# A decoder block on one core: ten of eleven tile pairs of the second feed-forward product in a seven-product form, in two passes, with the weight sums on GpSimd

## The reference

```python
def swiglu_ffn(x, g, w_in, w_out):
    h = rmsnorm(x, g)
    gate, up = jnp.split(h @ w_in, 2, axis=-1)
    return x + (jax.nn.silu(gate) * up) @ w_out        # hidden width 2816, w_out is 2816 x 1024
```

## Time and profile before

| | before |
|---|---|
| median of 3 runs | 900.63 us (900.39 to 900.72) |
| profiled execution | 900.4 us, its span 898.7 us |
| TensorE busy | 888.4 us (99%) |
| VectorE busy | 596.2 us (66%) |
| ScalarE busy | 385.7 us (43%) |
| GpSimd busy | 57.5 us (6%) |
| mean granted TensorE clock | 0.999 |

### The profile page before, as it was taken

The page is one execution under the profiler, slowest core; times in us unless marked ns, Lnnn a source line. Parts: engine busy times, 40 slices in busy tenths (PEclk is TensorE's granted clock), DMA queues, the critical chain, the costliest instruction groups (busy, mean ns, idle before and its releaser), DMA issues.

```text
span 898.7 us, 13165 instructions
## 1 busy us (share of the span) xinstructions
PE 888.4 (99%) x5292; PEld 793.1 (88%) x5292; DVE 596.2 (66%) x711; ACT 385.7 (43%) x555; POOL 57.5 (6%) x59
## 2 busy tenths in 40 slices
PE   9999999999999999999999999999999999999997
PEld 7998888889999998988888888899999999888886
DVE  5685666789577678755466476998888887433333
ACT  5654432345444444523244332554555445322223
POOL 0111000000000000024100053000000000000000
PEclk9999999999999999999999999999999999999999
DMA  9946332213322222672211122222322233322212
GB/s 350 364 168 265 110 105 94 94 47 99 137 93 95 94 100 89 226 289 94 92 49 51 44 94 107 81 95 97 127 103 93 93 116 117 117 93 94 94 48 94
DMA packets 16091, 108.17 MB, mean 120 GB/s; under 512 B 1840, under 2 KB 1968, under 8 KB 4016
## 3 DMA queue, kind: packets, MB, share of 16 engines
q1 hardware_dynamic: 13408, 93.99, 28.3%
q10 hardware_dynamic: 2176, 12.00, 3.5%
q0 software_dynamic: 464, 1.57, 0.5%
HBM read 101.26 MB, written 6.29 MB: 120 GB/s over the span
## 4 chain that ended last, share of the span: by engine, by line
PE 84%; DVE 10%; ACT 4%; issue 2%; DMA 1%; SPq 0%; POOLq 0%; POOL 0%; ACTq 0%; DVEq 0%
PE psum L1445 28%; PE psum L1447 27%; PE psum L1446 27%; DVE blk L870 2%; ACT blk L395 1%; DVE sig L1155 1%; DMA pack<-first 1%; DVE tl L870 1%; DVE wl L870 1%; DVE raw L1061 1%; DVE raw L1059 1%; DVE raw L1060 1%; DVE merged L1158 0%; ACT wh L395 0%; PE psum L1697 0%
## 5 line engine op out<-in xcount | busy, mean ns | idle before, releaser
L1445 PE MATMUL psum<-th,w7h 128*128 128x256 f32 x504 | 142.7, 283 | 0.3 <-ACT snap L395 0.3
L1447 PE MATMUL psum<-th,w7l 128*128 128x256 f32 x504 | 142.6, 283 | 0.0
L1446 PE MATMUL psum<-tl,w7h 128*128 128x256 f32 x504 | 142.6, 283 | 0.0
L870 DVE TENSOR_TENSOR wl<-raw,wh 128x2048 fp32r<-128x2048 f32 (+1 forms) x44 | 89.4, 2043 | 50.0 <-ACT wh L395 49.9
L1445 PEld LDWEIGHTS psum<-th,w7h 128*128 128x128 f32 x504 | 96.8, 192 | 0.6 <-issue 0.5
L1446 PEld LDWEIGHTS psum<-tl,w7h 128*128 128x128 f32 x504 | 96.8, 192 | 0.0
L1447 PEld LDWEIGHTS psum<-th,w7l 128*128 128x128 f32 x504 | 96.8, 192 | 0.0
L395 ACT ACTIVATE wh<-raw 128x2048 fp32r<-128x2048 f32 (+1 forms) x44 | 73.1, 1675 | 20.8 <-PE psum L1447 19.5
L1445 PE MATMUL psum<-hh,wh 128*128 128x512 f32 x192 | 75.0, 391 | 0.0
L1447 PE MATMUL psum<-hh,wl 128*128 128x512 f32 x192 | 74.7, 389 | 0.0
L1446 PE MATMUL psum<-hl,wh 128*128 128x512 f32 x192 | 74.7, 389 | 0.0
(11 more groups left out here) (265 smaller groups left out, 2197.3 us busy)
## 6 DMA issues: line engine op xcount, KB each, us to landing
raw<-weights SPq DMA_DIRECT2D x79, 1024.0 KB, 4.8
pack<-first SPq DMA_DIRECT2D x3, 768.0 KB, 7.9
vraw<-weights SPq DMA_DIRECT2D x2, 1024.0 KB, 12.1
xt<-xt SPq DMA_DIRECT2D x1, 2048.0 KB, 18.7
X<-x SPq DMA_DIRECT2D x2, 1024.0 KB, 27.7
X<-x ACTq DMA_DIRECT2D x1, 2048.0 KB, 10.1
memt<-memt SPq DMA_DIRECT2D x1, 1024.0 KB, 22.6
kv_store<-kh ACTq DMA_DIRECT2D x1, 1024.0 KB, 3.9
```

The costliest lines, as they stand in the source:

```text
L870: return V.tensor_tensor(dst, v, f32(hi), ALU.subtract)
L1445: nc.tensor.matmul(dst, lh, rh, start=start, stop=False, **kw)
L1446: nc.tensor.matmul(dst, lh, rl, start=False, stop=False, **kw)
L1447: return nc.tensor.matmul(dst, ll, rh, start=False, stop=stop, **kw)
```

## The change

Of the eleven pairs, ten (`NP`) are now done in the seven-product form. For a pair, the 512 tokens are cut into halves of 256 and the 1024 columns into halves of 512, so that both the hidden values (two tiles x two halves of tokens) and the weights (two tiles x two halves of columns) are 2 x 2 blocks. Each product is 256 tokens x 128 x 512 columns: two output tiles x three matmuls, 42 matmuls for a pair. The results of the seven products need more room than PSUM has, so there are two passes over the ten pairs. Pass one does three products for every pair, into banks 4 and 5, 6 and 7, 0 and 1; pass two does the other four. Between and behind the passes, sums are kept in SBUF (`kept`) and added back (`merge_part`). The eleventh pair runs as before, with other bank numbers, once `fo_merged` says that its bank has been put together.

The weights are stored as four blocks per pair (`out_blocks`). Pass one loads the first three blocks, pass two the last three, 768 KB each time. GpSimd makes two sums of 128 x 512 for each pair and pass, in `raw` and in `t2` (`t2_early`, `t2_late`), 40 in all. The high and low parts are made in smaller pieces. VectorE also makes two sums of hidden values (128 x 256) per pair and pass.

The residual's 32 transposes now go into banks 2 and 3 during pass one, and ScalarE copies six of the eight results into `xres`; the last two stay in the banks. In the mixer's gates, the fourth `merge` of a half moves behind `gate_prep`. Semaphores of single use are joined into counting ones (`squares_ready`, `var_ready`, `rstd_ready`).

```diff
@@ GpSimd @@
+            for i in range(NP):
+                n = FO0 + i
+                w = raw[:, n % SLOTS, :]
+                pool.wait_ge(landed[n % SLOTS], landing(n))
+                nc.gpsimd.tensor_tensor(w[:, S:2 * S], w[:, S:2 * S], w[:, 0:S], ALU.subtract).then_inc(fo_sums, 1)
+                if i == 2:
+                    pool.wait_ge(panel_done, FO0)
+                    pool.dma_start(gf[:], gf_in.to_broadcast([P, D])).then_inc(gf_here, 16)
+                pool.wait_ge(fo_sums, 2 * i + 1)
+                nc.gpsimd.tensor_tensor(t2(i), w[:, 2 * S:3 * S], w[:, S:2 * S], ALU.subtract).then_inc(fo_sums, 1)
+            for i in range(NP):
+                n = FB0 + i
...
+                nc.gpsimd.tensor_tensor(w[:, 0:S], w[:, 3 * S:4 * S], t2(i), ALU.subtract).then_inc(fo_sums, 1)
+                nc.gpsimd.tensor_tensor(w[:, S:2 * S], w[:, 2 * S:3 * S], w[:, S:2 * S], ALU.subtract).then_inc(fo_sums, 1)
@@ ScalarE @@
+            def first_pass_hi(i):
+                p = i % SLOTS
+                act.wait_ge(hid_ready, 2 * i + 2)
+                act.wait_ge(panel_done, FO0 + i - 1)
+                copy(hsh[p][:, 0, 0:Q], hid[:, 2 * i, 0:Q]).then_inc(hid_first_hi, 1)
+                act.wait_ge(fo_sums, 2 * i + 1)
+                copy(foh[p][:, 0:2 * S], raw[:, p, 0:2 * S]).then_inc(fo_first_hi, 1)
...
+            def second_pass_hi(i):
+                p = i % SLOTS
+                act.wait_ge(panel_done, FB0 + i - 1)
+                copy(hsh[p][:, 1, :], hid[:, 2 * i + 1, :]).then_inc(hid_first_hi, 1)
+                act.wait_ge(fo_sums, 2 * NP + 2 * i + 2)
+                copy(foh[p][:, 0:2 * S], raw[:, p, 0:2 * S]).then_inc(fo_first_hi, 1)
@@ VectorE, gates @@
                 merge(h - 1, 2)
+                gate_prep(n + 1, i + 1)
                 merge(h - 1, 3)
-                gate_prep(n + 1, i + 1)
                 gate_prep_lo(n + 1, i + 1)
@@ VectorE @@
+            def first_pass_lo(i):
+                p = i % SLOTS
+                dve.wait_ge(hid_first_hi, i + 1)
+                lo(hsl[p][:, 0, 0:Q], hid[:, 2 * i, 0:Q], hsh[p][:, 0, 0:Q]).then_inc(hid_first_lo, 1)
+                chain(V.tensor_tensor(hid[:, 2 * i, Q:S], hid[:, 2 * i, Q:S], hid[:, 2 * i + 1, Q:S], ALU.add))
+                V.tensor_tensor(hid[:, 2 * i, 0:Q], hid[:, 2 * i, Q:S], hid[:, 2 * i, 0:Q], ALU.subtract).then_inc(hid_sums, 1)
+                dve.wait_ge(fo_first_hi, i + 1)
+                lo(fol[p][:, 0:2 * S], raw[:, p, 0:2 * S], foh[p][:, 0:2 * S]).then_inc(fo_first_lo, 1)
...
@@ TensorE @@
+            for i in range(NP):
+                p, last = i % SLOTS, i == NP - 1
+                done = fo_part if last else None
+                pe.wait_ge(hid_first_lo, i + 1)
+                pe.wait_ge(fo_first_lo, i + 1)
...
+                out_product(4, p, 0, 0, start=i == 0, signal=done)
+                pe.wait_ge(hsl_ready, i + 1)
+                out_product(6, p, 2, 1, start=i == 0, signal=done)
+                pe.wait_ge(lo_ready, FO0 + i + 1)
...
+                out_product(0, p, 1, 2, start=i == 0, signal=done, closing=True).then_inc(panel_done, 1)
```

More of the change, by code:

```diff
@@ L69 @@
 FO0 = FI0 + HT
-PANELS = FO0 + HT // 2
+NP = 10
+FB0 = FO0 + NP
+FC0 = FB0 + NP
+PANELS = FC0 + 1
 C_MEM, C_MIX, C_X, C_FFN = 0, 8, 16, 24
@@ L827, in _ @@
[L827 to L831 removed]
+            flat = lambda t: t[:].rearrange("p a b -> p (a b)")
+            def first_pass_hi(i):
[5 more added lines that the diff above has]
+                copy(foh[p][:, 0:2 * S], raw[:, p, 0:2 * S]).then_inc(fo_first_hi, 1)
@@ new lines, in second_pass_rest_hi, with keep_part @@
+            def second_pass_rest_hi(i):
+                p = i % SLOTS
+                copy(foh[p][:, 2 * S:4 * S], raw[:, p, 2 * S:4 * S]).then_inc(hi_ready, 1)
+                act.wait_ge(hid_sums, NP + i + 1)
+                copy(hsh[p][:, 0, :], hid[:, 2 * i, :]).then_inc(hsh_ready, 1)
+            def keep_part(which, product, src):
+                for m in range(2):
+                    act.wait_ge(*part_done(product, m))
+                    copy(kept[:, which, m, :], bank[src + m]).then_inc(fo_kept, 1)
@@ L1419, in _, with merge_part @@
+            def merge_part(b, product, which, m, kept_by=0):
+                dve.wait_ge(*part_done(product, m))
+                if kept_by:
+                    dve.wait_ge(fo_kept, kept_by)
+                src = kept[:, which, m, :] if which is not None else xres[:, m, :]
+                V.tensor_tensor(bank[b], bank[b], src, ALU.add).then_inc(fo_merged, 1)
             add_kept(0, NS - 2)
-            fo_lo(0)
+            first_pass_lo(0)
             strassen_product(0, NS - 2, hid[:, HT - 2, :])
@@ L1806, in _ @@
                 strassen_panel(it * 2 + 1, 1)
[L1808 to L1832, removed]
-                        elif n == HT // 2 - 1:
-                            ins.then_inc(fo_tile, 1)
@@ new lines, in out_product @@
+            def out_product(banks, p, a, w, start=False, signal=None, free=None, closing=False):
+                h, g = hsh[p][:].rearrange("p a b -> p (a b)"), hsl[p][:].rearrange("p a b -> p (a b)")
+                c = slice(w * S, (w + 1) * S)
+                for m in range(2):
+                    if free:
+                        pe.wait_ge(free[0], free[1] + m)
+                    r = slice(a * Q + m * P, a * Q + (m + 1) * P)
+                    ins = mm3(bank[banks + m], h[:, r], g[:, r], foh[p][:, c], fol[p][:, c], start, signal is not None, skip_group_check=True)
+                    if signal and not (m == 1 and closing):
+                        ins.then_inc(signal, 1)
+                return ins
```

262 lines of the change are left out of this document (197 added, 65 removed).

## The result

| | before | after |
|---|---|---|
| median | 900.61 us (900.39 to 900.72) | 910.37 us (910.18 to 912.53) |
| profiled execution | 900.4 us, its span 898.7 us | 910.2 us, its span 908.4 us |
| TensorE busy, matmuls | 888.4 us, 5292 | 885.2 us, 5232 |
| VectorE busy, instructions | 596.2 us, 711 | 677.4 us, 825 |
| GpSimd busy | 57.5 us | 126.2 us |

The ratio is 1.0114, 95% interval 1.0097 to 1.0132: the change makes the kernel 1.1% slower, clear of the noise. 60 matmuls are gone, 13.6 us at their rate, but TensorE's busy time falls by 3.2 us only. A matmul shows 0.39 us and starts every 0.227 us, so short gaps between them count as busy.

What follows compares the result with a forecast made beforehand. Before, TensorE's matmul count and issue rate bound the kernel; after, VectorE, held by GpSimd's sums, bounds the last stage. Stage 10.3 us longer less 1.6 in the gates, 8.7 us on 900.4: 909 us, range 897 to 918.

Steps and rivals of the forecast that it cites:

- 60 matmuls less are 13.6 us, if nothing holds TensorE.: Last stage, ten pairs: 48 matmuls become 42 each, 60 x 0.227 = 13.6 us less for TensorE.
- VectorE stands still for 1.10 us per sum.: Last stage: each GpSimd sum reading SBUF holds VectorE's two-input instructions 1.10 us, 2.20 us a pair and pass.
- No hold: Rival, last stage: GpSimd's sums barely hold VectorE, TensorE sets the pace; 885 to 893 us, about 887; chance 0.15.
- a short hold: Rival, last stage: a sum holds VectorE only 0.84 us, 9.4 us less, about 900 us; chance 0.12.
- I counted 36: Last stage: the number of GpSimd sums by which the prediction scaled the length of a hold on VectorE.
- VectorE becomes the bound in both passes, 5.69 and 6.38 us a pair.: Last stage: VectorE's work plus 2.20 us of holds exceeds TensorE's 4.09 us (pass one) and 5.45 us (pass two).
- VectorE over 90% busy: Sign that the hold is real: VectorE over 90% busy from 771 to 886 us.
- The stage is 10.3 us longer.: Last stage: TensorE begins the last of ten pairs at 885.7, ends 892.3; the eleventh began at 882.0 before.
- The gates gain 1.6 us.: Mixer's gates: moving the fourth merge behind gate_prep removes TensorE's three waits for `gsnap`, 1.6 us in total.
- The slot's round does not bind.: Last stage: landing, GpSimd sums, ScalarE copy and VectorE part take 8.2 us and waits, against 11.4 for two pairs.
- waits that end with a landing: Sign of being wrong: TensorE's waits ending with a DMA landing would mean the slot's round binds.
- GpSimd comes last: Rival, last stage: sums run only once VectorE has run dry; 8 us more, 917 us; chance 0.13.

Runs made afterwards that it cites:

- e1: The changed kernel with GpSimd's 40 sums replaced by memsets that read nothing in SBUF, the weight sums left out: 886.99 us, ratio 0.9848.
- e5: The changed kernel with 17 more GpSimd subtractions of two 128 x 512 SBUF tiles, into a spare tile nobody reads: 926.79 us, ratio 1.0293.
- e6: The changed kernel with 30 of GpSimd's 40 sums over 256 columns instead of 512: 898.51 us, ratio 0.9977.
- e7: The changed kernel loading one 256 KB block per pair and pass instead of 768 KB: 909.71 us, ratio 1.0096.

## Why the prediction was right

I predicted 909.0 us and 910.4 came out. By the steps:

- *60 matmuls less are 13.6 us, if nothing holds TensorE.* Shown in the main by e1. 887.0 us is 13.6 us under before, but some 2 us of that come from the gates. From the stage's first matmul or transpose to the eleventh pair TensorE takes 101.0 us in e1 (767.24 to 868.25) and 112.6 before (769.38 to 882.0): the stage gives 11.6. Of the 2.0 us that are missing, start to start, 1.4 are lost at the change of pass (811.00 to 812.62), 0.3 before the eleventh pair and 0.2 at 780.14.
- *VectorE stands still for 1.10 us per sum.* The size was right: 1.09 us on `hsl` of 512 (1.77 against 0.68), 1.10 us on a 1024 (2.32 at 769.87, against 1.22), and 1.10 us on an `hsl` of 256 (1.51 at 795.40, against 0.41). That reads hold and writes don't, that the cost goes by the number of reads and by their length, is shown by e1, e5 and e6. "No hold" and "a short hold" are refuted. The number of holds was wrong: I counted 36. VectorE is busy for 29.4 us longer than in e1 (677.4 against 648.0), where it does the same work without holds, and that is 27.
- *VectorE becomes the bound in both passes, 5.69 and 6.38 us a pair.* Measured 5.75 us (TensorE's starts from 782.83 to 817.33, six pairs) and 6.34 us (6.93 with a kept sum, forecast 6.99). In pass two its shape was right too. In pass one it was not: I expected VectorE over 90% busy all along, and it is 81% there, because some sums run while VectorE waits, and hold nobody. The numbers agree since 2.27 us of idle time take the place of two holds. Over both passes 10.3 us of idle time stand where nine holds, 9.9 us, are missing. I had not worked that out: it is luck. Nor had I seen that TensorE's own pace in pass one is 4.56 us and not 4.09; VectorE's is longer than either.
- *The stage is 10.3 us longer.* TensorE begins the eleventh pair at 891.66. As the gates shift all of it by 2.3 us (VectorE reaches `hsl` of the second pair at 768.74, where the kernel before is free at 771.0), that is 893.9 in the time of before, against 882.0: **11.9 us**. Of the 1.6 us too little, 0.6 came by the end of pass one (VectorE at 818.31, forecast 820.0 - 2.3 = 817.7). The rest I put down to the change of pass, below.
- *The gates gain 1.6 us.* Mis-sized: 2.3 to 2.8 us. The two misses nearly cancel: 11.9 - 2.3 = 9.6 us, for a measured 9.8.
- *The slot's round does not bind.* Right for pass two, wrong for pass one, where I had named waits that end with a landing as a sign of being wrong. Each of the three gaps of 2.27 us there, and the one at the change of pass, goes back to a landing. For the first, the slot is free at 774.49; the sum starts with the landing at 778.68 and takes 1.55 us, ScalarE's copy of 1024 takes 1.06, and VectorE's three parts, with two holds, run from 781.36 to 786.09, when the slot is free again. That is 11.6 us, where I had set 8.2: I had put 0.6 us for the copy and 0.6 us for VectorE's part, and left the holds out. VectorE's own work with all its holds is 11.4 us for two pairs, so the two limits lie side by side, and that they do is luck as well. In e7 with landings 1.1 us sooner the round is eased, and pass one still goes at 5.71 us a pair (783.90 to 818.15): VectorE waits less (4.1 us, not 6.8) and is held more (16 us, not 11).
- *GpSimd comes last*: not in the changed kernel, but in e6, in three pairs of e7 and once in e5. It deserved its chance, and the forecast had no ground to tell which would come.

**The change of pass** is what I left out. ScalarE (copies) and then GpSimd there:

```profile
822.08 2.00 ACT L433 ACTIVATE foh<-raw 128x1024 fp32r<-128x1024 f32 x2 [4.32 <-POOL raw L425]
```

```profile
819.14 1.66 POOL L424 TENSOR_TENSOR raw<-raw,t_early 128x512 f32<-128x512 f32 x1 [4.77 <-DMA raw<-weights]
820.76 1.28 POOL L425 TENSOR_TENSOR raw<-raw 128x512 f32<-128x512 f32 x1
822.73 1.27 POOL L424 TENSOR_TENSOR raw<-raw,t_early 128x512 f32<-128x512 f32 x1 [0.69 <-DMA raw<-weights]
```

Pass two's first sum needs a landing that comes at 819.14; in pass one ScalarE only needed one sum before its big copy, now it needs both, and VectorE waits 3.51 us for it. The bill is smaller than the wait: two sums of 1.10 us ran in that time and held nobody, so by my estimate the wait costs about 3.5 - 2.2 = 1.3 us; no run takes it away by itself. TensorE's 3.49 us of idle time there is the same stall seen from the other side and must not be added to it.

## What to carry to other kernels

Before giving work to GpSimd because it is idle, count VectorE's instructions that read two tiles in SBUF: beside them a GpSimd read is charged to VectorE, here at 1.10 us for a sum that VectorE does itself in 0.60. If VectorE's own work plus the holds passes TensorE's time for the same tiles, matmuls saved are worth nothing, as the 60 here were. And the size of a gap on TensorE is read from start to start and not from the wait that is shown.

## What the runs showed of the hardware that I had not expected

The hold goes by the length of GpSimd's read: 1.10 us for 512 columns, 0.55 us for 256, whatever the length of VectorE's instruction. A hold is shorter than the GpSimd instruction is shown (1.27 us and more). GpSimd's own rows stretch to 2.27 us, in e6 to 3.55 us and in e7 to 4.71 us, when it is the one that waits. Whether a waiting sum gets in between two VectorE instructions or only when VectorE has run dry, no run here decides.

After TensorE had stood idle its clock fell. The stretches before, at and after the change of pass, in the changed kernel:

```profile
821.00:825.00 4.00, 0.69 (x4) 0.23 (x2) 1.83 (x1) 2.92 (x5) 3.31 (x3) 1.00 0.23 95
826.00:829.00 3.00, 3.00 (x10) 2.49 (x9) 3.00 (x4) 2.57 (x5) 0.22 (x1) 0.50 0.16 45
832.00:835.00 3.00, 3.00 (x14) 2.46 (x14) 3.00 (x3) 0.63 (x1) 3.00 (x2) 1.00 0.39 119
```

From 826 to 829 the granted clock is 0.50, the lower level of 1.2 GHz, and matmuls start 0.43 us apart in place of 0.23; before and after it is full. Six matmuls lose about 1.2 us in this way. It costs the kernel nothing that I can show, since VectorE is busy without a break from 823.17 to 886.3 and is the bound. In e7 the clock fell in the same way after waits of 2.09, 1.97 and 2.19 us (at 773.39, 806.53 and 885.59), and its mean over the span is 0.993, so its 909.7 us are not quite free of this.
